# Attended values of a 16-head decoder taken out of one PSUM bank four heads at a time, with the last transposes moved up

## The chip, the cores and the metric

The kernel runs on one core of one Trainium2 chip. The time is device microseconds of one execution. Three runs of the kernel before gave 1002.4 to 1002.56 us, median 1002.46.

## What is computed

A decoder trunk of two layers on 256 tokens of width 1024, in float32. Each layer is a half-weight SwiGLU block, a mixing stage, and a second half-weight SwiGLU block. The mixing stage has 16 heads of width 64: eight with a relative bias over the top 64 keys of an indexer, eight with a forgetting bias.

```python
def token_mixing(h, w_in, b_forget, g_ckv, w_uk, w_uv, w_out, rel_bias):
    ...
    o_a = dsa_attention(q_a, c_kv, q_i, k_i, w_i, w_uk, w_uv, rel_bias)
    o_f = fox_attention(qkv_f[:, :, 0], qkv_f[:, :, 1], qkv_f[:, :, 2], log_f)
    o = jnp.concatenate([o_a.reshape(b, s, H_DSA * HEAD_DIM), o_f.reshape(b, s, H_FOX * HEAD_DIM)], axis=-1)
    return o @ w_out
```

Inside both attentions a head's logits go through a softmax, and the probabilities are multiplied with its values. The change touches the end of this: probabilities times values, and the product with `w_out`.

## The kernel before, in words

Every engine has its own program, written out by hand, and they meet through semaphores. PE does all products. Float32 is kept by splitting each factor into a high part (float32r) and a low part: three matmuls per product, high by high, low by high, high by low (`three`, lines 626 to 628). The weights come as a stream of chunks from HBM by SP's DMA queue. ACT makes the high part of a chunk (`split_front`, line 373, `split_back`, line 377), DVE the low part (lines 1103 and 1109).

The sixteen heads of the mixing stage are worked in eight rounds p of two heads. A round on the five engines:

- PE `logits(p)` (lines 867 to 874): queries by keys of two heads, 64 rows of the array each, into two PSUM banks.
- DVE `maxima` (line 1253): adds the bias, scales, and takes the row's extreme, for each of the two heads.
- ACT `probs` (lines 459 and 461): the exponentials of each head, with their sums.
- POOL `share` (lines 315 and 318): divides by the sum.
- PE `turn(hh)` (line 883): three transposes of a head's probabilities into the PSUM bank TURNB. It waits until POOL has divided, and until DVE has copied the head before out of that bank.
- DVE `turned(hh)` (line 1259): copies them to `prT`, which has room for two heads.
- PE `attend(p)` (lines 895 and 899): probabilities by values, two heads side by side in 64 columns of the array each, into 256 columns of the bank PVB. It waits until the round before is out of the bank.
- ACT `out_high(p)` (line 467): the high part of the attended values, 128x256, PVB to `ohi`. DVE `out_low(p)` (line 1263): the low part, to `olo`.
- PE `project(k, b)` (lines 626 to 628, six matmuls of 512 columns): attended values of round k, half b of the tokens, times their rows of `w_out`. It waits for `out_low` of that round.

PE's order is written as a list of these calls: between the logits and the turns it puts other products (columns of the forgetting heads' keys, their values, later the projections), so that PE does not stand while the other engines work. The other engines' orders are two loops over p from 0 to 9 in `mix`, with the splits of the next chunks placed at fixed rounds. On ACT three of those splits wait for projections to be done, so that the buffer they overwrite is free:

```python
                    if p == 8:
                        act.wait_ge(wo_mm, l * 2 * KT + 10)
                        front(12)
                        act.wait_ge(wo_mm, l * 2 * KT + 12)
                        back(12)
```

`wo_mm` is counted up by each `project`, so 12 is the end of `project(5, 1)`. Chunk 12 is the first of the next SwiGLU block.

Of the kernel before, what the change touches and what calls it, by code (L numbers as in the profile page):

```python
# [17 lines left out]
F32 = mybir.dt.float32  # L18
# [63 lines left out]
def trunk(nc, x, stream, final_gain, consts, rel_bias, out, table):  # L82
    with ExitStack() as ctx:
# [80 lines left out]
        onehot_r = ohi[0:NBUCKET, 0:2, :].rearrange("p a t -> p (a t)")[:, 0:TAB]  # L164
        rbhi, rblo = (olo[0:NBUCKET, 0, i * NH:(i + 1) * NH] for i in range(2))
        tab = prT[0:NH, 0, :]


        ps = ctx.enter_context(nc.psum_tensor("ps", [P, 8, 512], F32))
# [198 lines left out]
        def _(act):  # L368
# [77 lines left out]
            def mix(l):  # L446
# [6 lines left out]
                def probs(hh):  # L453

                    act.wait_ge(lg_out, l * 2 * NH + hh + 1)
                    t = hh % 4
                    if hh >= 4:
                        act.wait_ge(tr_mm, l * 2 * NH + hh - 3)
                    nc.scalar.activation(pr[:, t, 0:P], lg[:, t, 0:P], ACT.Exp, bias=nm[:, t, 0:1],
                                         scale=-1.0, accum_out=rsum[:, 0, hh:hh + 1])  # L460
                    nc.scalar.activation(pr[:, t, P:S3], lg[:, t, P:S3], ACT.Exp, bias=nm[:, t, 1:2],
                                         scale=-1.0, accum_out=rsum[:, 1, hh:hh + 1]).then_inc(pr_out, 1)

                def out_high(p):

                    act.wait_ge(pv_mm, l * NPAIR + p + 1)
                    nc.scalar.copy(ohi[:, p, :], ps[:, PVB, 0:S]).then_inc(othi_out, 1)

                def query_out(j):

# [79 lines left out]
                tile_low(7)  # L550

                for p in range(NPAIR + 2):
                    if p >= 2:
                        out_high(p - 2)
                    if p < NPAIR:
                        probs(2 * p)
                        probs(2 * p + 1)
                    if p == 0:
                        act.wait_ge(feat_mm, l * NFEAT + (FX + 5))
                        front(7)  # L560
                        act.wait_ge(feat_mm, l * NFEAT + (FX + 6))
                        back(7)
                    if p == 1:
                        act.wait_ge(feat_mm, l * NFEAT + NFEAT)
                        front(8)
                        back(8)
                    if p == 3:
                        act.wait_ge(vf_mm, l * 2 * 4 + 2 * 2)
                        front(9)
                    if p == 4:  # L570
                        act.wait_ge(vf_mm, l * 2 * 4 + 2 * 4)
                        for b in range(NB):
                            nc.scalar.mul(val[:, b, D // 2:D], ps[:, VALB + b, :], rstd[:, b:b + 1]).then_inc(vf_out, 1)
                        back(9)
                    if p == 5:
                        front(10)
                        back(10)
                    if p == 6:
                        act.wait_ge(wo_mm, l * 2 * KT + 4)
                        front(11)  # L580
                    if p == 7:
                        act.wait_ge(wo_mm, l * 2 * KT + 6)
                        back(11)
# [5 lines that stand above are left out]
# [34 lines left out]
        def _(pe):  # L623
# [176 lines left out]
            def mix(l):  # L800
# [44 lines left out]
                def project(k, b, s, at):  # L845

                    a = ohi[:, k, b * P:(b + 1) * P], olo[:, k, b * P:(b + 1) * P]
                    for j in range(2):
                        t = three(ps[:, 2 * b + j, :], a, w(s, at + j * 512, 512), k == 0, k == KT - 1)
                        if k == KT - 1 and j == 0:  # L850
                            t.then_inc(acc_mm, 1)
                    t.then_inc(wo_mm, 1)
# [33 lines left out]
                def attend(p):  # L886

                    pe.wait_ge(prT_out, l * 2 * NH + (2 * p + 2))
                    if p:
                        pe.wait_ge(otlo_out, l * NPAIR + p)  # L890
                    if p == NH // 2:
                        pe.wait_ge(vf_out, l * NB + NB)
                    for i in range(2):
                        v = slice((2 * p + i) * HD, (2 * p + i + 1) * HD)
                        nc.tensor.matmul(ps[i * HD:(i + 1) * HD, PVB, 0:S], val[:, 0, v], prT[:, i, 0:S],  # L895
                                         start=True, stop=False)
                    for i in range(2):
                        v = slice((2 * p + i) * HD, (2 * p + i + 1) * HD)
                        t = nc.tensor.matmul(ps[i * HD:(i + 1) * HD, PVB, P:S], val[:, 1, v], prT[:, i, S:S3],  # L899
                                             start=False, stop=True)  # L900
                    t.then_inc(pv_mm, 1)

                def token_major():
# [98 lines left out]
                turn(1)  # L1002

                logits(2)
                attend(0)
                s = front(7)
                value(0, 0, s, 0)
                value(0, 1, s, 0)
# [2 lines left out]
                turn(3)  # L1011

                logits(3)
                attend(1)
                value(1, 1, s, UNIT)
                back(7)
# [3 lines left out]
                turn(5)  # L1020

                logits(4)
                attend(2)
                s = front(8)
                value(3, 0, s, 0)
                turn(6)
# [1 line left out]
                turn(7)  # L1028

                logits(5)  # L1030
                attend(3)
                s = front(9)
                pe.wait_ge(otlo_out, l * NPAIR + 1)
# [6 lines left out]
                turn(9)  # L1040

                logits(6)
                attend(4)
                project(1, 1, s, UNIT)
                back(9)
                pe.wait_ge(otlo_out, l * NPAIR + 3)
# [3 lines left out]
                turn(11)  # L1050

                logits(7)
                attend(5)
                s = front(10)
                pe.wait_ge(otlo_out, l * NPAIR + 4)
                project(3, 0, s, 0)
                project(3, 1, s, 0)
                turn(12)
                pe.wait_ge(otlo_out, l * NPAIR + 5)
                project(4, 0, s, UNIT)  # L1060
                turn(13)

                project(4, 1, s, UNIT)
                attend(6)
                back(10)
                pe.wait_ge(otlo_out, l * NPAIR + 6)
                project(5, 0, s, FRONT)
                turn(14)
                project(5, 1, s, FRONT)
                turn(15)  # L1070

                s = front(11)
                pe.wait_ge(otlo_out, l * NPAIR + 7)
                project(6, 0, s, 0)
                attend(7)
                project(6, 1, s, 0)
                back(11)
                pe.wait_ge(otlo_out, l * NPAIR + 8)
# [18 lines left out]
        def _(dve):  # L1097
# [123 lines left out]
            def mix(l):  # L1221
                def front(m, halves=(0, 1)):
                    split_front(l, NF + m, used=MIX_USED[m][0] if m < MIXC else FRONT, halves=halves)
# [32 lines left out]

                def turned(hh):
                    dve.wait_ge(tr_mm, l * 2 * NH + (hh + 1))
                    nc.vector.tensor_copy(prT[:, hh % 2, :], ps[:, TURNB, 0:S3]).then_inc(prT_out, 1)

                def out_low(p):
                    dve.wait_ge(othi_out, l * NPAIR + (p + 1))
                    nc.vector.tensor_tensor(olo[:, p, :], ps[:, PVB, 0:S], ohi[:, p, :].bitcast(F32), ALU.subtract
                                            ).then_inc(otlo_out, 1)

                def tile_out(j, bank=GU):

# [88 lines left out]
                for p in range(NPAIR + 2):  # L1356
                    if p < NPAIR:
                        maxima(2 * p)
                        maxima(2 * p + 1)
                    if p >= 2:  # L1360
                        out_low(p - 2)
                    if p == 0:
                        tile_out(FX + 4, FILLB)
                        front(7)
                        tile_out(FX + 5, FILLB)
                    if p == 1:
                        back(7)
                        tile_out(FX + 6, FILLB)
                        turned(0)
                        tile_out(FX + 7, FILLB)  # L1370
                        turned(1)
                    if p == 2:
                        front(8)
                        back(8)
                    if p == 4:
                        front(9, (0,))
                    if p == 6:
                        front(10, (0,))
                    if 2 <= p <= NPAIR:
                        turned(2 * p - 2)  # L1380
                        if p == 4:
                            front(9, (1,))
                        if p == 6:
                            front(10, (1,))
                        turned(2 * p - 1)
                    if p == 5:
                        back(9)
                    if p == 6:
                        back(10)
                    if p == 7:  # L1390
                        front(11)
                        back(11)
                    if p == 8:
                        front(12)
                back(12)
                dve.wait_ge(acc_mm, l * 8 + 4)
                residual(0, 0, 1.0)
# [141 lines left out]
```

## Time and profile before

| | |
|---|---|
| median of three runs | 1002.46 us |
| the profiled execution | 1003.15 us, of which span 1001.3 us |
| PE busy | 991.9 us (99% of the span), 5647 instructions |
| weight loads (PEld) busy | 844.6 us (84%) |
| DVE busy | 754.8 us (75%) |
| ACT busy | 538.8 us (54%) |
| POOL busy | 139.7 us (14%) |
| granted TensorE clock, mean | 0.998 |
| HBM traffic | 186 GB/s over the span |

The mixing stage of the first layer, from the first logits to the last projection, runs from 247.6 to 314.5 us; that of the second layer repeats it 492.1 us later. A busy share says only that an engine had work; where one engine is at 99%, what counts is each moment in which it would have to wait.

### The profile page before, as it was taken

The numbers are of one execution on the slowest core, as the hardware profiler recorded it, in microseconds if no ns is written. First come the engines' busy times: TensorE is split into PE (matmuls) and PEld (weight loads), VectorE is DVE, ScalarE is ACT, GpSimd is POOL, SyncE is SP. The second block draws the span as 40 slices with busy tenths as digits, with TensorE's granted clock in tenths as the row PEclk, the third lists the DMA queues.
The fourth block names the chain that finished last, engine by engine and source line by source line (L and its number), as shares of the span: only waits on it lengthen the run. The fifth ranks groups of instructions, "written<-read, shape, count | busy, mean of one in ns | idle before, by whom it ended". The sixth has DMA issues, their size and how long they took to land.

```text
span 1001.3 us, 16517 instructions
## 1 busy us (share of the span) xinstructions
PE 991.9 (99%) x5647; PEld 844.6 (84%) x5647; DVE 754.8 (75%) x1503; ACT 538.8 (54%) x977; POOL 139.7 (14%) x154
## 2 busy tenths in 40 slices
PE   9999999999999999999999999999999999999997
PEld 8888888888878888888888888889887788888885
DVE  5887777679667887777788777777786688777775
ACT  5555555565565555555455555555755555555553
POOL 2000000018761000000000000000297500000001
PEclk9999999999999999999999999999999999999999
DMA  8665555765534665555536555554563446555541
GB/s 303 209 198 188 189 186 189 250 230 179 199 107 151 219 196 189 189 189 189 189 130 213 195 186 187 187 185 149 185 214 129 170 149 221 190 189 189 189 147 43
DMA packets 38021, 184.76 MB, mean 185 GB/s; under 512 B 3888, under 2 KB 8160, under 8 KB 23776
## 3 DMA queue, kind: packets, MB, share of 16 engines
q1 hardware_dynamic: 33264, 178.60, 53.7%
q10 hardware_dynamic: 4720, 5.67, 1.8%
q8 instruction: 23, 0.38, 0.2%
q14 instruction: 14, 0.11, 0.0%
HBM read 183.18 MB, written 2.64 MB: 186 GB/s over the span
## 4 chain that ended last, share of the span: by engine, by line
PE 98%; DMA 1%; DVE 0%; POOL 0%; DVEq 0%; issue 0%
PE ps L632 33%; PE ps L633 17%; PE ps L626 13%; PE ps L628 12%; PE ps L627 12%; PE ps L718 1%; PE ps L642 1%; PE ps L883 1%; PE ps L646 1%; PE ps L643 1%; PE ps L895 1%; PE ps L874 1%; PE ps L870 1%; DMA cst<-consts 1%; PE ps L728 0%; PE ps L899 0%
## 5 line engine op out<-in xcount | busy, mean ns | idle before, releaser
L632 PE MATMUL ps<-xboth,whi 128*128 128x512 f32 x1440 | 508.0, 395 | 0.0
L633 PE MATMUL ps<-xboth,wlo 128*128 128x256 f32 x1440 | 403.4, 280 | 0.0
L632 PEld LDWEIGHTS ps<-xboth,whi 128*128 128x128 f32 x1440 | 269.9, 187 | 63.7 <-issue 1.0
L633 PEld LDWEIGHTS ps<-xboth,wlo 128*128 128x128 f32 x1440 | 272.0, 189 | 3.6
L1103 DVE TENSOR_TENSOR wlo<-raw,whi 128x1024 fp32r<-128x1024 f32 (+1 forms) x214 | 250.3, 1206 | 6.0 <-ACT whi L373 6.0
L373 ACT CAST whi<-raw 128x1024 fp32r<-128x1024 f32 (+1 forms) x222 | 217.5, 1029 | 7.4 <-PE ps L628 7.4
L1109 DVE TENSOR_TENSOR wlo<-raw,whi 128x1024 fp32r<-128x1024 f32 (+1 forms) x110 | 132.8, 1207 | 99.9 <-ACT whi L377 99.8
L413 ACT ACTIVATE sig<-hg 128x256 f32<-128x256 f32 x88 | 36.9, 419 | 198.5 <-DVE hg L1181 182.4
L377 ACT CAST whi<-raw 128x1024 fp32r<-128x1024 f32 (+1 forms) x112 | 112.8, 1007 | 53.4 <-PE ps L628 53.0
L628 PE MATMUL ps<-whi,hlo 128*128 128x512 f32 x352 | 138.9, 395 | 0.0
L627 PE MATMUL ps<-wlo,hhi 128*128 128x512 f32 x352 | 138.8, 394 | 0.0
L626 PE MATMUL ps<-whi,hhi 128*128 128x512 f32 x352 | 138.6, 394 | 0.0
L285 POOL TENSOR_TENSOR rstd<-ms,mhalf 128x1 f32<-128x1 f32 x14 | 13.6, 983 | 591.8 <-DVE ms L1120 591.4
L418 ACT CAST hhi<-hf 128x256 fp32r<-128x256 f32 x88 | 35.8, 406 | 98.2 <-DVE hf L1198 98.2
L628 PEld LDWEIGHTS ps<-whi,hlo 128*128 128x128 f32 x352 | 66.3, 188 | 15.3
L626 PEld LDWEIGHTS ps<-whi,hhi 128*128 128x128 f32 x352 | 66.3, 188 | 15.1
L627 PEld LDWEIGHTS ps<-wlo,hhi 128*128 128x128 f32 x352 | 66.3, 188 | 11.8
L1200 DVE TENSOR_TENSOR hlo<-hf,hhi 128x256 fp32r<-128x256 f32 x88 | 37.4, 426 | 41.6 <-ACT hhi L418 41.6
L626 PE MATMUL ps<-xboth,whi 128*128 128x256 f32 x160 | 46.5, 291 | 0.0
L627 PE MATMUL ps<-xboth,whi 128*128 128x256 f32 x160 | 45.2, 283 | 0.0
L628 PE MATMUL ps<-xboth,wlo 128*128 128x256 f32 x160 | 45.2, 283 | 0.0
L1186 DVE TENSOR_TENSOR ht<-ur,sig 128x256 f32<-128x256 f32 x88 | 37.5, 426 | 9.2
(175 smaller groups left out, 1189.5 us busy)
## 6 DMA issues: line engine op xcount, KB each, us to landing
raw<-stream SPq DMA_DIRECT2D x111, 1024.0 KB, 5.2
raw<-stream SPq DMA_DIRECT2D x113, 512.0 KB, 3.6
decay<-table ACTq DMA_DIRECT2D x2, 1024.0 KB, 8.4
table<-table ACTq DMA_DIRECT2D x1, 1524.0 KB
X<-x SPq DMA_DIRECT2D x2, 512.0 KB, 5.6
bias<-table ACTq DMA_DIRECT2D x1, 1024.0 KB, 5.7
cst<-consts SPq DMA_DIRECT2D x1, 576.0 KB, 11.1
raw<-stream SPq DMA_DIRECT2D x2, 256.0 KB, 6.4
```

The source lines that it names most:

```text
L373: nc.scalar.copy(whi[:, k % 2, at], raw[:, k % 2, at]).then_inc(hi_front, 1)
L377: nc.scalar.copy(whi[:, k % 2, FRONT:FRONT + used], raw[:, k % 2, FRONT:FRONT + used]).then_inc(hi_back, 1)
L413: nc.scalar.activation(sig[:, s, :], hg[:, s, :], ACT.Sigmoid).then_inc(sig_out, 1)
L626: nc.tensor.matmul(out_, a[0], b[0], start=start, stop=False)
L627: nc.tensor.matmul(out_, a[0], b[1], start=False, stop=False)
L628: return nc.tensor.matmul(out_, a[1], b[0], start=False, stop=stop)
L632: nc.tensor.matmul(ps[:, bank, :], a[0], xboth[:, k, :], start=k == 0, stop=False)
L633: return nc.tensor.matmul(ps[:, bank, 0:S], a[1], xhi[:, k, :], start=False, stop=k == KT - 1)
L1103: nc.vector.tensor_tensor(wlo[:, s, at], raw[:, s, at], whi[:, s, at].bitcast(F32), ALU.subtract).then_inc(w_front, 1)
L1109: nc.vector.tensor_tensor(wlo[:, s, at], raw[:, s, at], whi[:, s, at].bitcast(F32), ALU.subtract).then_inc(w_back, 1)
L1186: nc.vector.tensor_tensor(ht[:, s, :], ur[:, s, :], sig[:, s, :], ALU.mult).then_inc(ht_out, 1)
L1200: nc.vector.tensor_tensor(hlo[:, s, :], hf[:, s, :], hhi[:, s, :].bitcast(F32), ALU.subtract).then_inc(hlo_out, 1)
```

## The change

Attended values of rounds 2q and 2q+1 now go into the two halves of PVB, and are taken out together:

- `attend` of an even round moves behind the logits of the next, directly ahead of `attend` of the odd round: 0 and 1 behind `logits(3)`, 2 and 3 behind `logits(5)`, 4 and 5 behind `logits(7)`, 6 and 7 between the two halves of project 5.
- `out_high` and `out_low` are called for every second round with 128x512 and count their semaphores up by two. On ACT, `out_high(p - 3)` stands behind the `probs` of round p, and the last, `out_high(6)`, falls in pass 9 of the loop. On DVE, `out_low` stands ahead of the `turned` calls of odd rounds; the last is called after the loop, ahead of `front(12)`.
- The transposed probabilities of odd rounds go to two idle tiles of the SwiGLU block, `sig` and `hg` (`turned_at`).
- `turn(12)` to `turn(15)` move up: one behind each half of projects 3 and 4.

```diff
+        turned_at = [prT[:, i, :] for i in range(2)] + [t[:, :, :].rearrange("p a t -> p (a t)")[:, 0:S3] for t in (sig, hg)]
...
                 def out_high(p):
-                    act.wait_ge(pv_mm, l * NPAIR + p + 1)
-                    nc.scalar.copy(ohi[:, p, :], ps[:, PVB, 0:S]).then_inc(othi_out, 1)
+                    act.wait_ge(pv_mm, l * NPAIR + p + 2)
+                    nc.scalar.copy(ohi[:, p:p + 2, :].rearrange("p a t -> p (a t)"), ps[:, PVB, :]).then_inc(othi_out, 2)
...
                 for p in range(NPAIR + 2):
-                    if p >= 2:
-                        out_high(p - 2)
                     if p < NPAIR:
                         probs(2 * p)
                         probs(2 * p + 1)
+                    if p % 2 and p > 1:
+                        out_high(p - 3)
...
                 def attend(p):
                     pe.wait_ge(prT_out, l * 2 * NH + (2 * p + 2))
-                    if p:
+                    if p and p % 2 == 0:
                         pe.wait_ge(otlo_out, l * NPAIR + p)
...
                 logits(7)
+                attend(4)
                 attend(5)
                 s = front(10)
                 pe.wait_ge(otlo_out, l * NPAIR + 4)
                 project(3, 0, s, 0)
+                turn(12)
                 project(3, 1, s, 0)
-                turn(12)
+                turn(13)
                 pe.wait_ge(otlo_out, l * NPAIR + 5)
                 project(4, 0, s, UNIT)
-                turn(13)
-
+                turn(14)
                 project(4, 1, s, UNIT)
-                attend(6)
+                turn(15)
                 back(10)
                 pe.wait_ge(otlo_out, l * NPAIR + 6)
                 project(5, 0, s, FRONT)
-                turn(14)
+                attend(6)
+                attend(7)
                 project(5, 1, s, FRONT)
-                turn(15)
                 s = front(11)
                 pe.wait_ge(otlo_out, l * NPAIR + 7)
                 project(6, 0, s, 0)
-                attend(7)
                 project(6, 1, s, 0)
...
                 def turned(hh):
                     dve.wait_ge(tr_mm, l * 2 * NH + (hh + 1))
-                    nc.vector.tensor_copy(prT[:, hh % 2, :], ps[:, TURNB, 0:S3]).then_inc(prT_out, 1)
+                    nc.vector.tensor_copy(turned_at[hh % 4], ps[:, TURNB, 0:S3]).then_inc(prT_out, 1)
                 def out_low(p):
-                    dve.wait_ge(othi_out, l * NPAIR + (p + 1))
-                    nc.vector.tensor_tensor(olo[:, p, :], ps[:, PVB, 0:S], ohi[:, p, :].bitcast(F32), ALU.subtract
-                                            ).then_inc(otlo_out, 1)
+                    dve.wait_ge(othi_out, l * NPAIR + (p + 2))
+                    high, low = (t[:, p:p + 2, :].rearrange("p a t -> p (a t)") for t in (ohi, olo))
+                    nc.vector.tensor_tensor(low, ps[:, PVB, :], high.bitcast(F32), ALU.subtract).then_inc(otlo_out, 2)
...
-                    if p >= 2:
-                        out_low(p - 2)
+                    if p % 2 and 1 < p < NPAIR:
+                        out_low(p - 3)
...
-                    if p == 8:
-                        front(12)
+                out_low(NPAIR - 2)
+                front(12)
                 back(12)
```

The instruction list of ACT at the end of the mixing stage (layer 1), from the `probs` of round 7 on. L467 is `out_high`, L373 and L377 are the splits of the weight chunks. Before:

```order
L461 ACTIVATE pr,rsum<-lg,nm 128x256
L377 CAST whi<-raw 128x1024 [waits back_in1,wo_mm]
L467 CAST ohi<-ps 128x256 [waits pv_mm]
L373 CAST whi<-raw 128x1024 [waits front_in0,wo_mm]
L373 CAST whi<-raw 128x1024
L377 CAST whi<-raw 128x1024 [waits back_in0,wo_mm]
L467 CAST ohi<-ps 128x256 [waits pv_mm]
```

The same place in the changed kernel, whose lines are one higher here:

```order
L462 ACTIVATE pr,rsum<-lg,nm 128x256
L468 CAST ohi<-ps 128x512 [waits pv_mm]
L378 CAST whi<-raw 128x1024 [waits back_in1,wo_mm]
L374 CAST whi<-raw 128x1024 [waits front_in0,wo_mm]
L374 CAST whi<-raw 128x1024
L378 CAST whi<-raw 128x1024 [waits back_in0,wo_mm]
L468 CAST ohi<-ps 128x512 [waits pv_mm]
```

The cast of rounds 4 and 5 now stands directly behind the last `probs`. Of rounds 6 and 7 none is left ahead of the last L378; the one cast of both stands behind it.

DVE from the `maxima` of round 7 on (layer 1). L1263 is `out_low`, L1259 `turned`. Before:

```order
L1253 ISA nm 128x1
L1263 TENSOR_TENSOR olo<-ps,ohi 128x256 [waits othi_out]
L1259 COPY prT<-ps 128x384 [waits tr_mm] x2
L1103 TENSOR_TENSOR wlo<-raw,whi 128x512 [waits hi_front] x2
L1109 TENSOR_TENSOR wlo<-raw,whi 128x1024 [waits hi_back]
L1263 TENSOR_TENSOR olo<-ps,ohi 128x256 [waits othi_out]
L1259 COPY prT<-ps 128x384 [waits tr_mm] x2
L1103 TENSOR_TENSOR wlo<-raw,whi 128x1024 [waits hi_front] x2
L1263 TENSOR_TENSOR olo<-ps,ohi 128x256 [waits othi_out]
```

In the changed kernel:

```order
L1254 ISA nm 128x1
L1265 TENSOR_TENSOR olo<-ps,ohi 128x512 [waits othi_out]
L1260 COPY prT<-ps 128x384 [waits tr_mm] x2
L1104 TENSOR_TENSOR wlo<-raw,whi 128x512 [waits hi_front] x2
L1110 TENSOR_TENSOR wlo<-raw,whi 128x1024 [waits hi_back]
L1260 COPY sig<-ps 128x384 [waits tr_mm]
L1260 COPY hg<-ps 128x384 [waits tr_mm]
L1265 TENSOR_TENSOR olo<-ps,ohi 128x512 [waits othi_out]
L1104 TENSOR_TENSOR wlo<-raw,whi 128x1024 [waits hi_front] x2
```

The first `out_low` here now covers rounds 4 and 5 instead of round 5, and still stands ahead of the copies of heads 12 and 13; the copies of heads 14 and 15 stand behind the same three weight splits as before.

## Rows read from the trace of the kernel before

**Rows 1.** Page, part 4: shares of the chain of waits that ended last, by engine.
```profile
PE 98%; DMA 1%; DVE 0%; POOL 0%; DVEq 0%; issue 0%
```
**Rows 2.** Waits of PE, whole span: waiting line, releaser, us in total, times, longest.
```profile
PE ps L654 <- DVE chi L1406: 1.3, 1, 1.3
PE ps L718 <- DVE spare L1411: 0.6, 1, 0.6
```
**Rows 3.** Timeline of PE, attend behind logits: start us, us, line, tiles, shapes, count.
```profile
289.00 0.60 PE L874 MATMUL ps<-feat 64*128 64x256 f32 x4
289.53 0.65 PE L895 MATMUL ps<-prT,val 128*64 128x256 f32 x4
...
290.33 0.51 PE L626 MATMUL ps<-whi,ohi 128*128 128x512 f32 x1
290.67 0.39 PE L627 MATMUL ps<-wlo,ohi 128*128 128x512 f32 x1
290.90 0.40 PE L628 MATMUL ps<-whi,olo 128*128 128x512 f32 x1
```
**Rows 4.** Timeline of PE, logits with no attend behind them.
```profile
255.54 0.60 PE L874 MATMUL ps<-feat 64*128 64x256 f32 x4
...
256.29 0.28 PE L627 MATMUL ps<-xboth,whi 128*128 128x256 f32 x1
256.41 0.28 PE L628 MATMUL ps<-xboth,wlo 128*128 128x256 f32 x1
```
**Rows 5.** Timeline of PE, attend between two projections.
```profile
303.20 0.40 PE L628 MATMUL ps<-whi,olo 128*128 128x512 f32 x1
303.53 0.65 PE L895 MATMUL ps<-prT,val 128*64 128x256 f32 x4
...
304.67 0.40 PE L627 MATMUL ps<-wlo,ohi 128*128 128x512 f32 x1
```
**Rows 6.** Timeline of PE, one attend in windows that cut its second pass off or into.
```profile
296.27 0.44 PE L895 MATMUL ps<-prT,val 128*64 128x256 f32 x2
...
296.27 0.65 PE L895 MATMUL ps<-prT,val 128*64 128x256 f32 x3
```
**Rows 7.** Timeline of PE, first matmul behind attend(5), then turns 12, 13, 15.
```profile
297.07 0.50 PE L626 MATMUL ps<-whi,ohi 128*128 128x512 f32 x1
...
299.98 0.49 PE L883 MATMUL ps<-cst,pr 128*128 128x128 f32 x3
...
301.71 0.49 PE L883 MATMUL ps<-cst,pr 128*128 128x128 f32 x3
...
307.56 0.49 PE L883 MATMUL ps<-cst,pr 128*128 128x128 f32 x3
```
**Rows 8.** ACT: timeline rows; then a group by form (count, busy us, mean ns, idle).
```profile
299.72 1.03 ACT L377 CAST whi<-raw 128x1024 fp32r<-128x1024 f32 x1
...
307.76 1.05 ACT L377 CAST whi<-raw 128x1024 fp32r<-128x1024 f32 x1 [1.05 <-PE ps L628]
...
L535 ACT COPY val<-ps 128x512 f32<-128x512 f32 x4 | 2.2, 644 | 0.0
```
**Rows 9.** DVE: timeline rows; then a group by form.
```profile
293.77 0.56 DVE L1259 COPY prT<-ps 128x384 f32<-128x384 f32 x1 [0.70 <-PE ps L883]
...
302.23 0.56 DVE L1259 COPY prT<-ps 128x384 f32<-128x384 f32 x1 [1.17 <-PE ps L883]
...
305.05 0.42 DVE L1263 TENSOR_TENSOR olo<-ps,ohi 128x256 fp32r<-128x256 f32 x1
...
L1163 DVE SCALAR_TENSOR_TENSOR X<-ps,X 128x512 f32<-128x512 f32 x24 | 16.6, 692 | 4.7 <-PE ps L628 4.6
```
**Rows 10.** Timeline of PE at the program's start: warming matmuls of one shape.
```profile
1.34 4.42 PE L654 MATMUL ps<-chi 128*128 128x256 f32 x19 [1.34 <-DVE chi L1406]
...
7.58 1.21 PE L654 MATMUL ps<-chi 128*128 128x256 f32 x8
```
**Rows 11.** Busy us and count per engine in one window, then granted clock, DMA share, GB/s.
```profile
0.00:6.00 6.00, 4.42 (x19) 4.13 (x19) 0.51 (x3) 1.49 (x2) 0.34 (x6) 1.00 0.65 191
```

More of the change, by code:

```diff
@@ L892, in attend @@
                         pe.wait_ge(vf_out, l * NB + NB)
+                    at = p % 2 * S
                     for i in range(2):
                         v = slice((2 * p + i) * HD, (2 * p + i + 1) * HD)
-                        nc.tensor.matmul(ps[i * HD:(i + 1) * HD, PVB, 0:S], val[:, 0, v], prT[:, i, 0:S],
-                                         start=True, stop=False)
+                        nc.tensor.matmul(ps[i * HD:(i + 1) * HD, PVB, at:at + S], val[:, 0, v],
+                                         turned_at[p % 2 * 2 + i][:, 0:S], start=True, stop=False)
                     for i in range(2):
                         v = slice((2 * p + i) * HD, (2 * p + i + 1) * HD)
-                        t = nc.tensor.matmul(ps[i * HD:(i + 1) * HD, PVB, P:S], val[:, 1, v], prT[:, i, S:S3],
-                                             start=False, stop=True)
+                        t = nc.tensor.matmul(ps[i * HD:(i + 1) * HD, PVB, at + P:at + S], val[:, 1, v],
+                                             turned_at[p % 2 * 2 + i][:, S:S3], start=False, stop=True)
                     t.then_inc(pv_mm, 1)
@@ L1004, in mix @@
                 logits(2)
-                attend(0)
                 s = front(7)
@@ L1013, in mix @@
                 logits(3)
+                attend(0)
                 attend(1)
@@ L1022, in mix @@
                 logits(4)
-                attend(2)
                 s = front(8)
@@ L1030, in mix @@
                 logits(5)
+                attend(2)
                 attend(3)
@@ L1042, in mix @@
                 logits(6)
-                attend(4)
                 project(1, 1, s, UNIT)
```

## The prediction

> **What bounds the kernel now.** I read the chain of waits first: it runs through PE for 98% of the span [rows 1]. Then PE's own waits: two, 1.9 us in all, both at the program's start [rows 2]. So in the mixing stage PE never waits for another engine, and only two things can move the time: the time that PE's own instructions take, and a wait that is new. Third, I read PE's timeline around `attend` for the first, and ACT's and DVE's timelines at the end of the mixing stage for the second. All times below are of the first layer; the second repeats it.
>
> **What pairing saves on PE.** An `attend` works in 64-column tiles, the projections around it in full tiles, the logits in 64-row tiles. Changes of shape are what can be saved. With an `attend` behind the logits, from L874 to the second matmul of the projection are 290.67 - 289.00 = 1.67 us [rows 3]. With none it is 256.29 - 255.54 = 0.75 us in a place where the steady step is 256.41 - 256.29 = 0.12 [rows 4] instead of 290.90 - 290.67 = 0.23 [rows 3], so 0.86 us with matmuls of 512 columns. An `attend` behind logits costs 1.67 - 0.86 = 0.81 us. Between two projections it is 304.67 - 303.20 = 1.47 us [rows 5], less two steps of 0.235: 1.00 us, since there both changes of shape are its own.
>
> The second `attend` of a pair has no row. From below it costs its passes alone: a pass of 256 columns adds 0.65 - 0.44 = 0.21 us [rows 6], two of these and two of half the length give 0.64 us. From above it costs what a whole `attend` takes from its first matmul to the projection's, 290.33 - 289.53 = 0.80 us [rows 3]. I take 0.64, since the shape does not change and operands and lengths are the same; 0.80 stays as an end of the range.
>
> Per layer: three pairs behind logits save 2 x 0.81 - (0.81 + 0.64) = 0.17 each, the pair in project 5 saves 2 x 1.00 - (1.00 + 0.64) = 0.36. Sum **0.87 us per layer**. The logits that now have no `attend` behind them pay the change of shape that the 0.86 already holds. The turns keep their price: each still stands between two projections.
>
> **What PE's new order waits for.** PE comes to `logits(7)` early: five `attend` have become four, in two pairs, 5 x 0.81 - 2 x 1.45 = 1.15 us. Then the pair of rounds 4 and 5 costs 0.64 more than the single one, so project 3 starts at 297.07 [rows 7] - 1.15 + 0.64 = 296.56. Its first half takes six steps of 0.23 and a change of shape, 1.51, so `turn(12)` comes at 298.07. From turn to turn over half a projection it is 301.71 - 299.98 = 1.73 us [rows 7], so `turn(13)` is due at 299.80, 14 and 15 each 1.73 later.
>
> *First wait, turn(13).* It needs `turned(12)`, which stands on DVE behind `out_low(4)`, and that behind the cast on ACT, which now stands behind both `probs` of round 7. DVE works without a pause from `turned(10)` at 293.77 [rows 9] to the end of the `maxima` of round 7, and ACT's `probs` follow those; so all of it rides on PE's turns and comes 1.15 earlier. ACT was free at 299.72 [rows 8], now at 298.57. The cast of 512 columns has no row of its own; a copy of that shape out of PSUM takes 0.64 [rows 8]: 299.21. `out_low` of 512 columns: 0.69, as DVE's work of that shape on PSUM [rows 9]: 299.95 with 0.05 for the semaphore. `turned(12)`, 0.56 less 0.08 overlap with the instruction before it: 300.43, so `turn(13)` starts at 300.48. **PE waits 0.68 us.** The two-fold instruction is cheaper than two single ones, but what counts here is that it stands ahead of `turned(12)`, where half the work stood before, and that `turn(13)` moved close to `turn(12)`.
>
> *Second wait, turn(15).* `turn(14)` is now due at 302.21. `turned(13)` starts 0.53 behind its turn, 301.01. Three splits of chunk 11 stand behind it; they end at 305.05 - 302.23 = 2.82 us [rows 9] from its start, 303.83. Then `turned(14)`, 0.56: `turn(15)` starts at 304.44 instead of 303.94. **0.50 us.** Before, turns 14 and 15 came after these splits.
>
> *Third wait, project(6, 0).* From `turn(15)` to `attend(6)` it is 303.53 [rows 5] - 301.71 = 1.82 us, so 306.26. The pair takes 0.80 + 0.64, project(5, 1) starts at 307.70 and project(6, 0) is due 1.51 later, at 309.21. It needs rounds 6 and 7 out of PSUM. ACT's cast of them stands behind the split that waits for the end of project(5, 1): the row at 307.76 [rows 8], 0.20 after the point at which PE went on to `turn(15)`, 307.56 [rows 7]. So nothing of this chain can start before PE has run out of work. It is 0.20, the split's 1.05 [rows 8], the cast's 0.64, a semaphore 0.05, `out_low` 0.69, a semaphore 0.05: **2.68 us**. (ACT's instructions overlap by some 0.1; I leave that in for a first matmul after a wait, whose weights may not be loaded ahead.) Before, the cast of round 6 stood ahead of the splits of chunk 12, and the one of round 7 had a whole projection to run under.
>
> What is queued behind these waits: ACT's next split and DVE's splits of chunk 12 come later with PE. DVE ends them at about 315.1, before the first residual can start, some 3.5 us after project(6, 0) began at 311.9. They stay hidden. POOL's division for heads 14 and 15 is done before their turns. The weight transfers go into raw buffers that free up with the splits, and the next chunk is needed only after the norm. ACT and DVE have fewer instructions (two of 256 columns become one of 512), worth nothing: neither is the bound.
>
> **The sum.** Per layer -0.87 + 0.68 + 0.50 + 2.68 = +2.99 us, for two layers +6.0. The profiled execution took 1003.15, so it would be 1009.1; the median lies 0.7 lower, and from 1002.46 I get **1008.5 us**, 0.6% slower. A measurement of this kernel tells about 0.2%, 2 us, from no change.
>
> **The rivals.**
> *Only the last wait is real.* If DVE takes `turned(12)` and `turned(14)` in time, because ACT and DVE run further ahead than I think, per layer 2.68 - 0.87, in all +3.6: 1006.1 us. For it: both short waits are differences of sums of ten rows. Against: each queue is fixed, and both chains rest on measured ends.
>
> *The clock falls in the wait.* A PE that stands for 2.7 us twice is new here. At the program's start the same warming matmuls took 4.42/19 = 0.233 us each, later 1.21/8 = 0.151 with a turn's overhead in it [rows 10], and a pass of 256 columns takes 0.12 [rows 4]. So there PE ran at the lower of its two levels, 1.2 GHz, for 4.4 us, though the column of the granted clock shows 1.00 in that window too [rows 11]. If the wait set it back for as long, it would lose 2.2 us per layer: 1008.5 + 4.4 = 1012.9 us. Against: these 4.4 us follow a PE that had done nothing at all. The Trainium skill (TensorE: Matmul & The Clock Gate, section "Why this matters for your kernels") asks for no long gaps between bursts of matmuls, since the array then goes back to half its clock. No stretch of this trace has such a gap in the middle, so no row here shows how long is long.
>
> *Faster.* The three waits vanish and the saving stays: 1002.46 - 1.7 = 1000.7 us. The place is project(6, 0): it decides whether ACT can bring out rounds 6 and 7 before project(5, 1) is over. The chain would have to be shorter than the 0.87 us saved per layer; 2.68 is three times that, and nothing in ACT's queue lets the cast pass the split. If the shape changes saved more than I count, they would have to save four times as much.
>
> *It doesn't do what it says.* If two `attend` in a row drained the array between them, as between shapes, the second costs 0.80: 4 x 0.16 x 2 = 1.3 us more, 1009.8. That is inside the forecast's own range.
>
> **How the numbers follow.** The forecast 0.68, the last wait alone 0.12, the clock 0.12, faster 0.04, and 0.04 for sums that cancel to within 0.2% or a time in between. The range takes in the forecast with its bounds (0.80 for the second `attend`, 0.1 us more for each of six restarts: 1010.6) and the case of the last wait alone with 0.5 us for its rows: 1005.6 to 1010.8. It leaves out the clock and the faster case, 0.2 together. Faster by over 0.2%: 0.04; within: 0.03; slower: 0.93.
>
> **What would show it.** In PE's waits of the changed kernel three new rows per layer: transposes on DVE's copy of about 0.7 and 0.5 us, a projection's matmul on `olo` of about 2.6. In ACT's timeline the last cast of `ohi` directly behind a split that began with the end of project(5, 1). In PE's timeline, from the first matmul of one `attend` to the first of the next, 0.65 to 0.7 us. And the steps behind the long wait: 0.23 us if the clock holds, 0.43 or more if not. I am wrong if the last wait is under 1 us, or if the time between the second layer's start and the first's grows by anything but about 3 us.

## The result, and the profile after

The changed kernel takes 1009.39 us in the median of six executions (1008.90 to 1011.98), the kernel before 1002.51 in its six. The ratio is 1.0072, 95% interval 1.0062 to 1.0082: slower by 0.7%. The profiled execution took 1009.2 us, its span 1007.3. Here and below a ratio is estimated over all executions of both kernels in the fast state, which leaves out one of 1389 us of the kernel before, at a granted clock of 0.654, in each of the two groups of experiments. It need not equal the quotient of two medians; beside the experiments the kernel before had a median of 1002.8 us.

PE's waits over the whole span (waiting line, releaser, us in total, times, longest), which answer to [rows 2]:

```profile
PE ps L627 <- DVE olo L1265: 5.0, 2, 2.5
PE ps L655 <- DVE chi L1407: 1.3, 1, 1.3
PE ps L884 <- DVE prT L1260: 0.9, 2, 0.5
PE ps L884 <- DVE sig L1260: 0.8, 2, 0.4
PE ps L719 <- DVE spare L1412: 0.3, 1, 0.3
```

Three waits per layer are new: the projection on `olo`, two turns on DVE's copies. The list leaves out the tails of the matmuls before, whose modelled ends reach into the wait; how late a matmul starts is read from start to start. PE's timeline in layer 1: `attend(4)`, the first matmul of `attend(5)` and the first of project(3, 0); turns 12 to 15; the last matmul of project(5, 1) and the first two of project(6, 0).

```profile
294.78 0.65 PE L897 MATMUL ps<-prT,val 128*64 128x256 f32 x4
...
295.48 0.38 PE L897 MATMUL ps<-sig,val 128*64 128x256 f32 x1
...
296.23 0.50 PE L627 MATMUL ps<-whi,ohi 128*128 128x512 f32 x1
...
297.73 0.49 PE L884 MATMUL ps<-cst,pr 128*128 128x128 f32 x3
...
300.10 0.52 PE L884 MATMUL ps<-cst,pr 128*128 128x128 f32 x3 [0.47 <-DVE prT L1260]
...
301.85 0.49 PE L884 MATMUL ps<-cst,pr 128*128 128x128 f32 x3
...
304.16 0.52 PE L884 MATMUL ps<-cst,pr 128*128 128x128 f32 x3 [0.42 <-DVE sig L1260]
...
308.73 0.40 PE L629 MATMUL ps<-whi,olo 128*128 128x512 f32 x1
311.64 0.47 PE L627 MATMUL ps<-whi,ohi 128*128 128x512 f32 x1 [2.51 <-DVE olo L1265]
311.94 0.40 PE L628 MATMUL ps<-wlo,ohi 128*128 128x512 f32 x1
```

From turn to turn it should be 1.73 us [rows 7]. From 12 to 13 it is 2.37, so 0.64 late; from 14 to 15 it is 2.31, 0.58 late. Project(6, 0) starts 2.91 us after the matmul before it, where a step is 0.235: 2.68 late, and its first step takes 0.30 instead of 0.23. The second `attend` starts 0.70 us after the first, and from the pair's first matmul to the projection's it is 1.45 us, where a single `attend` takes 0.80 [rows 3].

ACT's timeline behind project(5, 1), which answers to [rows 8], and then DVE's:

```profile
309.17 1.04 ACT L378 CAST whi<-raw 128x1024 fp32r<-128x1024 f32 x1 [3.39 <-PE ps L629]
310.12 0.58 ACT L468 CAST ohi<-ps 128x512 fp32r<-128x512 f32 x1
```

```profile
310.80 0.69 DVE L1265 TENSOR_TENSOR olo<-ps,ohi 128x512 fp32r<-128x512 f32 x1 [5.53 <-ACT ohi L468]
```

ACT stands for 3.39 us until project(5, 1) has ended; then it makes the split, and only then the cast. Rounds 6 and 7 were ready in PSUM before: in e1_cast_first, below, whose times up to there are 0.02 us earlier, the cast starts at 307.61. So it comes 2.5 us later than it could. That is the chain of the forecast.

To compare stretches of two traces, I take the time from the norm's transposes before the mixing stage to those behind it (in the kernel before 196.46 to 314.50 us in layer 1). It is free of what differs at the program's start (this stretch begins between 195.7 and 196.5 us in the nine traces):

| kernel | mixing stage, layer 1 and 2, us | against before |
|---|---|---|
| before | 118.04, 118.04 | |
| changed | 121.26, 121.24 | +3.22, +3.20 |
| e1_cast_first | 119.01, 118.80 | +0.97, +0.76 |
| e2_copy_first | 118.64, 118.65 | +0.60, +0.61 |
| e3_turns_only | 117.97, 117.98 | -0.07, -0.06 |
| e4_both_copies | 117.49, 117.76 | -0.55, -0.28 |
| e6_attend_midway | 117.22, 117.23 | -0.82, -0.81 |
| e7_wait_in_between | 123.99, 122.20 | +5.95, +4.16 |
| e5_longer_wait | 125.37, 126.56 | +7.33, +8.52 |

The two SwiGLU blocks between the stages take 187.04 or 187.05 us each in every trace, so the whole loss lies in the stage. Part of what the table shows is not the changes' own: from the stage's start to the first logits (the first matmul of line 870 in the kernel before), where PE's order is the same in all kernels, it is 51.6 us in most layers but 51.86 in layer 1 of e1 and e7, layer 2 of e4 and both layers of e2. Why is open. From the first logits to the end of the stage both layers of a kernel agree within 0.01 us where the clock holds: 66.43 before, 69.65 changed (+3.22), 67.17 in e1 (+0.74), 66.77 in e2 (+0.34), 66.37 in e3 (-0.06), 65.89 in e4 (-0.54), 65.62 in e6 (-0.81). These are the numbers to compare.

### The profile page after: what moved, and what is told of

Same layout as the page of the kernel before. It is cut to its first block, busy times and chain, and to the rows that moved or that the text cites. A ratio compares the mean times of both kernels' runs of the same rounds, so it can differ in the third digit from the quotient of the medians.

```text
span 1007.3 us, 16509 instructions
## 1 busy us (share of the span) xinstructions
PE 991.4 (98%) x5647; PEld 844.0 (84%) x5647; DVE 754.0 (75%) x1495; ACT 537.9 (53%) x969; POOL 139.4 (14%) x154
## 4 chain that ended last, share of the span: by engine, by line
PE 96%; DVE 2%; DMA 0%; ACT 0%; issue 0%; POOL 0%; DVEq 0%; ACTq 0%
PE ps L633 33%; PE ps L634 17%; PE ps L627 12%; PE ps L629 12%; PE ps L628 12%; PE ps L719 1%; PE ps L643 1%; PE ps L647 1%; PE ps L644 1%; PE ps L884 1%; PE ps L897 1%; PE ps L875 1%; PE ps L871 1%; DVE wlo L1104 0%; DMA cst<-consts 0%
## 5 line engine op out<-in xcount | busy, mean ns | idle before, releaser
L378 ACT CAST whi<-raw 128x1024 fp32r<-128x1024 f32 (+1 forms) x112 | 112.8, 1007 | 58.6 <-PE ps L629 58.1
```

Of the source, the lines that this page charges most:

```text
L378: nc.scalar.copy(whi[:, k % 2, FRONT:FRONT + used], raw[:, k % 2, FRONT:FRONT + used]).then_inc(hi_back, 1)
```

## The experiments

The theory: pairing saves what the change says, and the order of the queues on ACT and DVE costs more. The rival: pairing itself is dear. A second rival, for the spread of the six executions, is taken up with the last two runs.

**The cast ahead of the split that waits (e1_cast_first).** The changed kernel with one call moved on ACT:

```diff
                         front(12)
+                        out_high(NPAIR - 2)
                         act.wait_ge(wo_mm, l * 2 * KT + 12)
                         back(12)
```

(and the loop's own call only for p under 8).

> The changed kernel with one call moved: on ACT the cast of rounds 6 and 7 (out_high(6)) stands ahead of the split of chunk 12's last third, which waits for the end of project(5, 1), instead of behind it. Queue-order theory: PE's wait of 2.5 us per layer ahead of project(6, 0) goes (under 0.2 left), the waits ahead of turn(13) and turn(15) stay at about 0.5 and 0.4 us; the span falls from 1007.3 by about 5 us to 1002.2, the time to about 1003.4, still over the kernel before by 0.9. Rival, that the time went into the pairing itself (drains, a slower array): the wait moves to another place or PE's own time stays up, and the time stays above 1007.

Measured: 1004.24 us (1003.75 to 1004.80), ratio to before 1.0013 [1.0004, 1.0022]. PE's waits of the mixing stage of layer 1:

```profile
PE ps L885 <- DVE prT L1261: 0.5, 1, 0.5
PE ps L885 <- DVE sig L1261: 0.4, 1, 0.4
```

The long wait is gone from the list and both short ones stand as they were. One call in ACT's queue was worth about 5 us of 6.9; project(6, 0) is still 0.20 us late, by its start. The rival falls. The median is 0.8 us above the expected time; by 0.3 us of that the kernel before was slower here too.

**The copy of head 12 ahead of out_low (e2_copy_first).** As e1, and on DVE in round 7 `out_low(4)` stands between `turned(12)` and `turned(13)`.

```diff
-                    if p % 2 and 1 < p < NPAIR:
+                    if p % 2 and 1 < p < NPAIR - 1:
                         out_low(p - 3)
...
                         if p == 6:
                             front(10, (1,))
+                        if p == NPAIR - 1:
+                            out_low(p - 3)
                         turned(2 * p - 1)
```

> As the one before, and on DVE the copy of head 12 stands ahead of out_low(4) instead of behind it. Queue-order theory: the wait ahead of turn(13) goes (0.5 to 0.6 us per layer), up to 0.15 us of it comes back ahead of project(4, 0), which needs out_low(4); turn(15) still waits about 0.4. Time about 1002.2, span 1001.0: no difference from the kernel before that can be told. Rival, that turn(13) waits for POOL's division or is too near to turn(12) whatever DVE does: the wait stays, the time as in the run before, 1003.4.

Measured: 1003.45 us (1003.06 to 1004.20), ratio 1.0004 [0.9995, 1.0014]. The wait of turn(13) is gone, so it came from DVE's order and not from POOL. But the one of turn(15), expected to stay at about 0.4, has grown, and the median is 1.2 us above the expected time:

```profile
PE ps L885 <- DVE sig L1261: 0.7, 1, 0.7
```

The reason stands in DVE's timeline, first of this kernel, from the copy of head 13 to that of head 14:

```profile
300.55 0.56 DVE L1261 COPY prT<-ps 128x384 f32<-128x384 f32 x1 [0.50 <-PE ps L885]
301.02 1.55 DVE L1105 TENSOR_TENSOR wlo<-raw,whi 128x512 fp32r<-128x512 f32 x2
302.50 1.21 DVE L1111 TENSOR_TENSOR wlo<-raw,whi 128x1024 fp32r<-128x1024 f32 x1
303.63 0.55 DVE L1261 COPY sig<-ps 128x384 f32<-128x384 f32 x1
```

In the changed kernel the same two half splits took 1.28 us. Turn(13) now comes 0.64 us earlier, counted from the first logits, and the copy of head 13 with it; with an unchanged way on DVE from there to the copy of head 14, turn(15) would come 0.64 earlier too. But that way is 3.08 us instead of 2.81. So 0.27 of the 0.64 us came back at the next wait, and about 0.4 is left in each layer.

**Both copies first (e4_both_copies).** As e2, and `turned(14)` between the splits of chunk 11:

```diff
                     if p == 7:
                         front(11)
+                        turned(2 * NPAIR - 2)
                         back(11)
```

(the loop's own call of it only for p under 8).

> As the one before, and on DVE the copy of head 14 stands ahead of the last split of chunk 11 instead of behind it. Queue-order theory: no wait over 0.15 us is left in the mixing stage, and what pairing saves shows alone: 0.87 us per layer by the sum, less 0.1 to 0.2 of small waits; span about 1000.0, time about 1001.3, below both kernels, 1.2 us (0.12%) under the kernel before. Rival, that a second attend in a row costs as much as a single one (0.80 us instead of 0.64 to 0.70): time 1002.4, as the kernel before. Rival, that the split now done later delays project(6, 0) on its weights: a wait on wlo there, time above 1002.5.

Measured: 1001.89 us (1001.40 to 1002.64), ratio 0.9991 [0.9982, 1.0000]. PE's list of waits holds none in the mixing stage any more. The interval reaches up to the kernel before, and the median is 0.6 us above the expected time. From the first logits on the gain is 0.54 us per layer instead of 0.87. PE's timeline says where most of the rest is: project(6, 0) starts 0.43 us after the matmul before it instead of 0.235, which the list of waits does not show, and its first step takes 0.31 instead of 0.23, together 0.27 us.

```profile
307.49 0.40 PE L630 MATMUL ps<-whi,olo 128*128 128x512 f32 x1
307.92 0.47 PE L628 MATMUL ps<-whi,ohi 128*128 128x512 f32 x1
308.23 0.39 PE L629 MATMUL ps<-wlo,ohi 128*128 128x512 f32 x1
```

**The last pair in the middle of project(5, 0) (e6_attend_midway).** As e4, and:

```diff
-                project(5, 0, s, FRONT)
-                attend(6)
-                attend(7)
+                project(5, 0, s, FRONT, lambda: (attend(6), attend(7)))
```

where `project` calls it between its two groups of three matmuls.

> The version with the cast and both copies moved, and attend(6) and attend(7) now between the two matmul groups of project(5, 0) instead of behind it, so that 0.7 us more of PE's work covers the way of rounds 6 and 7 out of PSUM. In the version without this, project(6, 0) still started 0.2 us late (PE's timeline), 0.27 with its slower first step. Queue-order theory: that goes, 0.5 us for two layers; time about 1001.4, span 999.6. Rival, that the 0.27 us is no wait but what a matmul costs behind an attend pair: the same time as that version, 1001.9.

Measured: 1001.25 us (1000.76 to 1001.54), ratio 0.9984 [0.9975, 0.9993]. This is faster than both kernels, by 0.16% than the one before; its whole interval lies on that side. The stage is 0.81 us shorter in each layer, the 0.27 us more than in e4, against 0.87 by the forecast's sum, and the start of project(6, 0) comes without a gap, 0.23 us behind the matmul before it:

```profile
307.76 0.40 PE L630 MATMUL ps<-whi,olo 128*128 128x512 f32 x1
307.99 0.40 PE L628 MATMUL ps<-whi,ohi 128*128 128x512 f32 x1
308.23 0.39 PE L629 MATMUL ps<-wlo,ohi 128*128 128x512 f32 x1
```

**The turns alone (e3_turns_only).** The kernel before, not paired; turns 12 and 13 behind the halves of project 3, turn 14 behind attend(6), turn 15 behind project(5, 0).

```diff
                 project(3, 0, s, 0)
+                turn(12)
                 project(3, 1, s, 0)
-                turn(12)
+                turn(13)
...
                 project(4, 0, s, UNIT)
-                turn(13)
                 project(4, 1, s, UNIT)
                 attend(6)
+                turn(14)
...
                 project(5, 0, s, FRONT)
-                turn(14)
+                turn(15)
                 project(5, 1, s, FRONT)
-                turn(15)
```

> The kernel before, unpaired, with turns 12 to 15 alone moved up: 12 and 13 behind the halves of project 3, 14 behind attend(6), 15 behind project(5, 0). Queue-order theory: turn(13) then comes 1.4 us earlier, but here out_low(4) is done long before and out_low(5) stands ahead of turned(12) with its cast ahead of both probs, so no copy is late: no wait over 0.1 us, time 1002.5 to 1002.8, as the kernel before. The short waits of the changed kernel then need both, the nearer turns and the paired instruction ahead of the copy. Rival, that nearer turns alone cost the 1.0 us per layer of the short waits: time about 1004.5.

Measured: 1002.55 us (1002.28 to 1002.96), ratio 0.9998 [0.9989, 1.0007], and no wait in the stage. Nearer turns by themselves cost nothing. In DVE's timeline `out_low(5)`, at 297.63 us, is over before the copy of head 12 is due:

```profile
297.63 0.41 DVE L1263 TENSOR_TENSOR olo<-ps,ohi 128x256 fp32r<-128x256 f32 x1
298.34 0.56 DVE L1259 COPY prT<-ps 128x384 f32<-128x384 f32 x1 [0.29 <-PE ps L883]
```

In the changed kernel `out_low(4)` came at 298.80 and the copy at 299.40. This run moves turns 14 and 15 less far than the change does, so for turn(15) it shows only that a copy behind the splits is in time when its turn comes later.

**A longer last wait (e5_longer_wait, e7_wait_in_between).** The changed kernel with three, and with one, more casts ahead of the last split:

```diff
                         act.wait_ge(wo_mm, l * 2 * KT + 12)
+                        act.wait_ge(back_in[0], arrivals(l, NF + 12))
+                        spent = decay[:, :, :].rearrange("p a t -> p (a t)")
+                        for i in range(3):
+                            nc.scalar.copy(spent[:, i * UNIT:(i + 1) * UNIT], raw[:, 0, FRONT:CHUNK])
                         back(12)
```

> The changed kernel with three more casts of 128x1024 on ACT (into a tile that is idle there) ahead of the last split of chunk 12: PE's wait ahead of project(6, 0) grows by 3 x 0.95 = 2.85 us to about 5.4 us per layer. If the array's clock does not react to a wait of this length: time 1009.4 + 5.7 = 1015.1, and the matmuls behind the wait start 0.23 us apart. If it falls: they start 0.43 us apart or more at first, and each layer loses up to 2.2 us more, time up to 1019.5; then the 2.5 us of the changed kernel was just short of it.

Measured: 1018.77 us (1018.43 to 1019.05), ratio 1.0158 [1.0143, 1.0174]. The waits grew as built, from 2.51 to 5.34 us, and the clock fell in both layers. PE's timeline behind the wait of layer 1:

```profile
314.46 0.77 PE L631 MATMUL ps<-whi,ohi 128*128 128x512 f32 x1 [5.34 <-DVE olo L1269]
315.02 0.63 PE L632 MATMUL ps<-wlo,ohi 128*128 128x512 f32 x1
315.45 0.63 PE L633 MATMUL ps<-whi,olo 128*128 128x512 f32 x1
...
317.48 0.40 PE L632 MATMUL ps<-wlo,ohi 128*128 128x512 f32 x1
317.71 0.40 PE L633 MATMUL ps<-whi,olo 128*128 128x512 f32 x1
```

Steps of 0.43 us, then of 0.23. The table by windows (busy us and count of PE, PEld, DVE, ACT, POOL, then granted clock, DMA share, GB/s) has the granted clock at 0.50 in the slow stretch, 1.2 GHz, the lower of the two levels:

```profile
314.40:317.10 2.70, 2.64 (x6) 2.15 (x7) 2.70 (x3) 0.00 (x0) 0.00 (x0) 0.50 0.00 0
```

Against the changed kernel with 2.85 us of casts added, 124.1 us, the stage lost 1.3 us more in layer 1 and 2.5 in layer 2, where the slow steps lasted longer (5 and 10 steps of 0.43). All four executions have the same mean clock, 0.993.

> The changed kernel with one more cast of 128x1024 ahead of the last split of chunk 12: PE's wait ahead of project(6, 0) becomes about 3.5 us per layer, between 2.5 (the changed kernel, where the clock fell in some executions by its granted mean of 0.995 and 0.996 instead of 0.998) and 5.3 (where it fell in every one, at a cost of 1.2 and 2.5 us in the two layers). Clock theory: 1009.2 + 1.9 = 1011.1 us where it holds, and up to 2.5 us per layer more where it falls, so executions spread from 1011 to 1016, more of them above than in the changed kernel. Rival, that the spread of the changed kernel has nothing to do with the length of the wait: all within 0.5 us of 1011.3.

Measured: 1014.04 us, four executions of 1013.25 to 1015.13, mean granted clock 0.996 to 0.994; ratio 1.0115 [1.0099, 1.0131]. In the one that was profiled, the fastest, the clock fell in one layer and not in the other, behind waits of the same 3.45 us; the fall cost 1.8 us (5.95, less 3.22 of the changed kernel and 0.94 by which the wait is longer). Layer 1, then layer 2:

```profile
313.21 0.47 PE L631 MATMUL ps<-whi,ohi 128*128 128x512 f32 x1 [3.45 <-DVE olo L1269]
...
314.50 0.63 PE L633 MATMUL ps<-whi,olo 128*128 128x512 f32 x1
314.92 0.63 PE L631 MATMUL ps<-whi,ohi 128*128 128x512 f32 x1
...
811.04 0.47 PE L631 MATMUL ps<-whi,ohi 128*128 128x512 f32 x1 [3.45 <-DVE olo L1269]
...
812.28 0.40 PE L633 MATMUL ps<-whi,olo 128*128 128x512 f32 x1
812.52 0.39 PE L631 MATMUL ps<-whi,ohi 128*128 128x512 f32 x1
```

The rival, that the spread has nothing to do with the wait, falls: none of the four is within 0.5 us of 1011.3. The clock theory fits the six executions of the changed kernel: four of 1008.90 to 1009.58 us with a mean clock of 0.998, one of 1010.52 with 0.996, one of 1011.98 with 0.995. The surplus of these two, 1.3 and 2.8 us, has the size of the losses above. Only the 0.998 execution of 1009.2 us was profiled, so that the clock fell behind the wait in the other two is a reading of their means, not of their traces.

## Why the prediction was right

The forecast was 1008.5 us, in a range of 1005.6 to 1010.8, slower with 0.93; measured were 1009.39. Its steps, per layer:

- *Pairing saves 0.87 us.* 0.81 in e6, where no wait hides it. The 0.64 for a second `attend` was right: a pair takes 1.45 us where a single one takes 0.80, so the second costs 0.65. The upper bound of 0.80 is out.
- *turn(13) waits 0.68.* 0.64 late, and gone with the order on DVE (e2).
- *turn(15) waits 0.50.* 0.58 late, gone when its copy passed the last split (e4).
- *project(6, 0) waits 2.68.* 2.68 late; with the cast ahead of the split it is 0.20 (e1). The parts were a little off and cancelled: the cast began 0.95 us after the split instead of 1.05, since the two overlap, and the projection 0.84 us after the start of `out_low` instead of 0.74. The prediction had not subtracted the overlap, to have something in hand for the first matmul behind a wait; that the two are equal was luck.
- *What is queued behind is hidden.* No wait on weights or residuals appeared; the SwiGLU block behind the stage takes 187.05 us as before.
- *The sum.* 2.99 forecast, 3.22 measured. Most of the rest is 0.08 us in turn(15), 0.06 saved less, and restarts (the first step behind the long wait takes 0.07 more, each of two turns behind a wait 0.02), less 0.04 in turn(13). For two layers the difference makes 0.5 of the 0.9 us between forecast and median. The clock makes 0.2 (next point); the last 0.2 is open. The top of the range holds a slip: 1008.5 with 1.3 for the second `attend` and 0.6 for the restarts is 1010.4, not 1010.6. Nothing hangs on it.
- *The clock.* I gave it 0.12 as a case in which it always falls. The runs point to something in between: two of the six executions have a lower mean clock, which lifts the median by 0.2 us (the other four have 1009.2) and the slowest to 1012, above the range. Had the clock fallen in most of them, the median would have been near the top of the range or over it, and no step of the prediction said that it would not: that part is luck. The cost was sized well (2.2 us per fall; 1.3, 1.8 and 2.5 measured). The Trainium skill (TensorE: Matmul & The Clock Gate, section "Why this matters for your kernels") says that stretches in which PE stands idle can throttle the clock again, and the trace agrees: here a wait of 3.45 us was followed by a lower clock in one of two layers, 5.34 us in both, and at 2.51 us the two executions with a lower mean clock point the same way.
- *Only the last wait is real*, 0.12: wrong, both short waits came.

What the forecast did not see is that an order of the same parts exists that wins. It priced the three waits as the change's; two belong to places in DVE's queue and one to a place in ACT's.

## What to carry to other kernels

When two small jobs are merged into one, the merged job runs at the time of the later one, and everything that stood behind the first is now behind both. Before the saving is counted, walk every queue in which the merged job stands: ask what stands ahead of it that waits for the very engine you want to keep busy, and what short copy behind it is needed first. Where a wait is removed, what stands behind it runs at another time and beside other work: here two splits became 0.27 us longer and gave part of the gain back. Price the chain to the end, and look at the next wait again.

## What the runs showed of the hardware

- The granted clock does not answer to the same wait in the same way each time: in one execution it fell behind one 3.45 us wait and not behind the other. It need not fall in the wait itself: in e7 four steps between matmuls were 0.23 to 0.31 us long before those of 0.43, while in e5 the first step was already 0.56. A fall cost 1.3 to 2.5 us.
- DVE's two splits of 128x512 take 1.28 us in the changed kernel, where they start at 301.13 us and POOL's last division is over at 300.86. They take 1.55 us in e2, e4 and e6, where they start 0.67 us earlier, counted from the first logits, and beside that division (in e2 it runs from 300.45 to 301.43, they start at 301.02). The longer splits in the trace of before (1.50 us for one of 128x1024 instead of 1.22) and in e3 (1.49 for the two, 1.63 for the next of 128x1024) lie beside POOL work too. That POOL is the cause was not tested.
- A matmul that started 0.20 us late (project(6, 0) in e1 and e4) did not appear in the list of waits at all, while PE's starts show it.
